# Weight chunks loaded as 112, 8 and 8 rows instead of 128

## The chip, the core and the metric

The kernel runs on one NeuronCore of a Trainium2 chip. The metric is the device time of one execution in microseconds. Before the change it is 1829.98 us, the median of three runs (1827.36 to 1831.81).

## The reference

The program computes a block of four mixers (convolution, short convolution, attention, recurrence) and an MLP, and then a second model of two layers on 16 meta tokens and 256 tokens of width 1024, all in float32. Nearly all of the time goes into the second part. Each of its layers ends in a retrieval of experts:

```python
def peer(h, w_query, sub_keys, u, v):
    # 8 heads, product keys (2 x 128 sub-keys), top-16 experts of 16384 for each head and token
    q = jnp.einsum('btd,dq->btq', hx, w_query)
    ...
    gate = jax.nn.softmax(best_s, axis=-1)
    u_sel = jnp.take(u, expert, axis=0)
    v_sel = jnp.take(v, expert, axis=0)
    act = jax.nn.gelu(jnp.einsum('btd,bthkd->bthk', hx, u_sel), approximate=False)
    return jnp.einsum('bthk,bthkd->btd', (gate * act), v_sel)
```

Between the two retrievals stand the key, value and query projections (w_kv, w_q), a stick-breaking attention, its output projection (w_o), and the queries of the second retrieval (peer_wq).

## The kernel before, in words

The 256 tokens are two tiles of 128. The retrieval of both layers is one loop over 32 units of 16 slots, 512 slots in all (`peer_gpsimd`, `peer_vector`, `peer_scalar`, `peer_tensor`). One slot is one expert for each of 128 pairs of token and head. GpSimd gathers for it 128 rows of 8 KB, the expert's u and v side by side (L634), into one of 8 buffers. VectorE multiplies the u half by the tokens' rows and sums (L675). ScalarE makes the gated weight from the sum (L706, L710). TensorE multiplies the weights with the v half (L662) and signals `v_used`, which frees the buffer for gather n + 8.

The work between the retrievals is spread over the same loop (`attend_pe`, `attend_act`, `attend_dve`), tile 0 beginning at step 34 of the 128 steps of four slots and tile 1 at step 66. Its weights come in chunks of 128 rows x 1024 columns, 512 KB: 48 chunks a tile (8 each for queries, keys, values and output, 16 for the retrieval's queries), 96 in all. They go through a ring of six buffers, `ring_w` (`RING_W`, L33). SyncE issues them in the order of their use: for chunk c >= 6 it first waits until TensorE has used chunk c - 6 (`w_used`), then issues one transfer (L1653) that adds 16 to the semaphore of that buffer. `product` (L821) waits on that semaphore for 16 times the number of chunks so far in this buffer, and then multiplies (L824, L828), at most one chunk ahead of each slot's value product in TensorE's order.

The same SyncE queue holds before these chunks the loads of the first block and of the keys, and after them the stores of the result (L1660), each behind a wait for its rows. All transfers, those of SyncE (queue 1), the gathers of GpSimd (queue 0) and the loads of instructions (queues 8 and 14), run on the same 16 DMA engines.

Other transfers that the prediction speaks of: the two loads of in_vectors, of 90 and 42 rows of 512 bytes (L1228, L1229); two loads of 16 rows of 4 KB (L1615, L1616); and eight copies of 16 rows of 4 KB within the SBUF (L1626).

Of the kernel before, what the change touches and what calls it, by code (L numbers as in the profile page):

```python
# [12 lines left out]
P = 128  # L13
# [19 lines left out]
RING_W = 6  # L33
# [19 lines left out]
def program(nc, x, vectors, w_in, lru_wa, lru_wx, w_out, post_mix_g, mlp_w1, mlp_w2, post_mlp_g, meta_tokens, norm_ffn,  # L53
            pool_w, pool_scale, w_kv, w_q, w_o, peer_wq, peer_keys, peer_uv, out):
    ctx = ExitStack()
    with ctx:
# [5 lines left out]
        def S(name):  # L62

            if name not in named:
                named[name] = nc.alloc_semaphore(name=name)
                count[name] = 0
            return named[name]
# [60 lines left out]
        def bank(b, n=1):  # L128
            return ps[:, BANK * b:BANK * (b + n)]
# [68 lines left out]
        ring_w = [big[:, W + D * i:W + D * (i + 1)] for i in range(RING_W)]  # L198
# [258 lines left out]
        def scores_ready(dve, u):  # L457

            if u == META_UNIT:
                return  # L460
            if u < L0_UNITS:
                dve.wait_ge(S("ffn0_scores_out"), u + 1)
            else:
                _, t, _, half = UNITS[u]
                dve.wait_ge(S("f_scores_out"), 2 * t + half + 1)
# [343 lines left out]
        def attend_tiles(t):  # L809

            return [X_TILES[0], META_TILE] if t == 0 else [X_TILES[1]]

        def product_done(engine, t, chunk):

            engine.wait_ge(S("w_used"), CHUNKS * t + chunk + KD)

        def product(pe, t, chunk, k, src, b, meta_bank=None):

            m = nc.tensor
            c = CHUNKS * t + chunk + k  # L820
            pe.wait_ge(S(f"w{c % RING_W}_loaded"), 16 * (c // RING_W + 1))  # L821
            w = ring_w[c % RING_W]
            for half in range(2):
                last = m.matmul(bank(b + half), src, w[:, BANK * half:BANK * (half + 1)],  # L824
                                start=(k == 0), stop=(k == KD - 1))
            if meta_bank is not None:
                for half in range(2):
                    last = m.matmul(bank(meta_bank)[TOK * half:TOK * (half + 1), :], kv_in[0][:, k, 0:TOK],  # L828
                                    w[:, BANK * half:BANK * (half + 1)], start=(k == 0), stop=(k == KD - 1))
            last.then_inc(S("w_used"), 1)  # L830

        def attend_pe(pe, t, i, q):
# [23 lines left out]
            for k in share(AT_Q, i)[q:q + 1]:  # L856
                product(pe, t, C_Q, k, q_in[:, k, :], 4)
# [4 lines left out]
            for k in share(AT_K, i)[q:q + 1]:  # L862
                product(pe, t, C_K, k, x_in[:, k, :], 6, 4 if t == 0 else None)
# [13 lines left out]
            for k in share(AT_V, i)[q:q + 1]:  # L877
                product(pe, t, C_V, k, x_in[:, k, :], 6, 4 if t == 0 else None)
# [118 lines left out]
        def attend_act(act, t, i):  # L997
# [13 lines left out]
            if i == AT_Q + 1:  # L1011
                if t == 1:
                    act.wait_ge(S("f_q_t"), 2)
                product_done(act, t, C_Q)
                a.activation(raw, bank(4, 2), ACT.Copy)
                a.activation(sq, bank(4, 2), ACT.Square).then_inc(S("a_raw"), 1)
            if i == AT_K + 1:
                product_done(act, t, C_K)
                act.wait_ge(S("a_scaled"), ONE["a_scaled"] * t + 1)
                if t == 0:  # L1020
                    a.activation(raw_m, bank(4)[0:HD], ACT.Copy)
                    a.activation(kn_m, bank(4)[0:HD], ACT.Square)
                a.activation(raw, bank(6, 2), ACT.Copy)
                a.activation(sq, bank(6, 2), ACT.Square).then_inc(S("a_raw"), 1)
# [23 lines left out]
            if i == AT_V + 1:  # L1048
                product_done(act, t, C_V)
                if t == 0:  # L1050
                    for half in range(2):
                        a.activation(v_meta[:, BANK * half:BANK * (half + 1)],
                                     bank(4)[TOK * half:TOK * half + META], ACT.Copy)
                a.activation(hn[:, t, :], bank(6, 2), ACT.Copy).then_inc(S("a_v_out"), 1)
# [552 lines left out]
        with nc.Block() as block:  # L1607
            @block.sync
            def _(sp):
                w1_v = mlp_w1[0].rearrange("(k p) n -> p k n", p=P)  # L1610
                w2_v = mlp_w2[0].rearrange("(f p) n -> p f n", p=P)
                wq_v = peer_wq[0].rearrange("(k p) n -> p k n", p=P)
                pool_v = pool_w[0].rearrange("g (k p) n -> p (g k) n", p=P)
                sp.dma_start(meta_poolw, pool_v).then_inc(S("meta_poolw_loaded"), 16)
                sp.dma_start(meta_scale, pool_scale[0].partition_broadcast(META)).then_inc(S("meta_gains_loaded"), 16)  # L1615
                sp.dma_start(meta_gain, norm_ffn[0].partition_broadcast(META)).then_inc(S("meta_gains_loaded"), 16)  # L1616
                sp.dma_start(w2b[1], w2_v[:, FT:2 * FT, :]).then_inc(S("w2_1_loaded"), 16)
                sp.dma_start(wq_peer, wq_v).then_inc(S("peer_wq0_loaded"), 16)
                sp.wait_ge(S("meta_mixed"), 1)
                sp.dma_start(meta_keys.rearrange("p j n -> p (j n)"), peer_keys[0]).then_inc(S("meta_keys_loaded"), 16)  # L1620
                for c in range(2, CHUNKS_MLP):
                    b = c % 2
                    if c == 3:
                        sp.wait_ge(S("meta_q_done"), 1)
                        for head in range(PH):
                            sp.dma_start(meta_x[META * head:META * (head + 1), :], meta_rows).then_inc(S("meta_x_loaded"), 16)  # L1626
                    sp.wait_ge(S("up_done"), FT * (c - 1))
                    sp.dma_start(w1b[b], w1_v[:, :, CHUNK * c:CHUNK * (c + 1)]).then_inc(S(f"w1_{b}_loaded"), 16)
                    sp.wait_ge(S("down_done"), FT * (c - 1))
                    sp.dma_start(w2b[b], w2_v[:, FT * c:FT * (c + 1), :]).then_inc(S(f"w2_{b}_loaded"), 16)  # L1630
                sp.wait_ge(S("meta_summed"), 1)
                sp.dma_start(wq_peer, wq_v).then_inc(S("peer_wq0_loaded"), 16)
                sp.wait_ge(S("up_done"), DFF // P - FT)
                sp.dma_start(scale_row, pool_scale[0].partition_broadcast(P)).then_inc(S("pool_w_loaded"), 16)
                sp.dma_start(poolw, pool_v).then_inc(S("pool_w_loaded"), 16)
                sp.wait_ge(S("mlp_done"), NT)
                sp.dma_start(ffn0_row, norm_ffn[0].partition_broadcast(P)).then_inc(S("ffn0_gain_loaded"), 16)
                sp.wait_ge(S("x2"), NT)
                sp.dma_start(gb[:, :, :].rearrange("p a n -> p (a n)"), peer_keys[0]).then_inc(S("keys0_loaded"), 16)
                sp.wait_ge(S("ffn0_scores_done"), L0_UNITS)  # L1640
                sp.dma_start(gb[:, 0, :], norm_ffn[1].partition_broadcast(P)).then_inc(S("gain0_loaded"), 16)

                kv_v, p_v = w_kv.rearrange("(k p) n -> k p n", p=P), peer_wq[1].rearrange("(k p) n -> k p n", p=P)
                q_v, o_v = (w[0].rearrange("(k p) n -> k p n", p=P) for w in (w_q, w_o))
                for c in range(NT * CHUNKS):
                    n, k = c % CHUNKS // KD, c % KD
                    if c == RING_W:
                        sp.wait_ge(S("experts_ready"), PH)
                        sp.dma_start(sc[:, 0:2 * PH * KEYS], peer_keys[1]).then_inc(S("keys1_loaded"), 16)
                    if c >= RING_W:  # L1650
                        sp.wait_ge(S("w_used"), c - RING_W + 1)
                    src = (q_v[k], kv_v[k, :, 0:D], kv_v[k, :, D:2 * D], o_v[k], p_v[k, :, 0:D], p_v[k, :, D:2 * D])[n]
                    sp.dma_start(ring_w[c % RING_W], src).then_inc(S(f"w{c % RING_W}_loaded"), 16)  # L1653

                out_v = out[0].rearrange("(t p) d -> p t d", p=P)
                for t in range(NT):
                    for g in range(QUADS):
                        r = slice(TOK * g, TOK * (g + 1))
                        sp.wait_ge(S("tile_out"), QUADS * (NT + t) + g + 1)
                        sp.dma_start(out_v[r, t, :], h[r, t, :]).then_inc(S("out_stored"), 16)  # L1660
                sp.wait_ge(S("out_stored"), 16 * NT * QUADS)
# [386 lines left out]
```

## Time and profile before

| what | value |
|---|---|
| median of 3 runs | 1829.98 us |
| profiled execution, first to last instruction | 1826.5 us |
| TensorE busy | 1366.8 us (75%) |
| VectorE busy | 1169.7 us (64%) |
| ScalarE busy | 597.3 us (33%) |
| GpSimd busy | 551.0 us (30%) |
| moved by DMA | 681.29 MB, mean 373 GB/s |
| mean granted TensorE clock | 0.843 |

The profile is of one execution. Its span leaves out what lies before the first and after the last instruction, so it is a little under the measured time. The page cuts the span into 40 slices of 45.7 us; a digit is the busy share in tenths. A DMA share of 1.00 or a little over means that the 16 engines have a packet in hand all the time. "A <- B" in the tables of waits means that the instruction A stood idle until B was done.

### The profile page before, as it was taken

The page shows a single profiled execution, that of the slowest core. Times are in us where ns is not written, and L with a number is a line of the kernel's source. Part 1 is how long each engine was busy: PE and PEld are TensorE (multiplying, and loading weights), DVE is VectorE, ACT ScalarE, POOL GpSimd, SP SyncE. Part 2 cuts the span into 40 slices and gives each one's busy share as a digit, 9 for nine tenths or more (in the row PEclk, how much of TensorE's full clock was granted, in tenths as well). Part 3 has the DMA queues.
Part 4 walks back from the last instruction along what each step waited for, and adds up shares of the span by engine and source line. Part 5 has one row for each costly group of instructions (what it writes and reads, how often), then busy time and mean ns, then how long its engine had stood idle before and what let it go on. Part 6 is the DMA issues. An engine that isn't in the chain of part 4 may idle for free.

```text
span 1826.5 us, 21618 instructions
## 1 busy us (share of the span) xinstructions
PE 1366.8 (75%) x7080; PEld 550.5 (30%) x7080; DVE 1169.7 (64%) x2705; ACT 597.3 (33%) x1530; POOL 551.0 (30%) x633
## 2 busy tenths in 40 slices
PE   8999999988874545698678865776787765655566
PEld 7856666653430010122122221221232210101011
DVE  5831334277776777656786647767877577677764
ACT  2421011124342323433443323433443333333332
POOL 2001232023332333322433224322342333333331
PEclk9999999999996676799777878897898977666677
DMA  9048697559999999999999999999999999999997
GB/s 358 5 176 345 204 373 263 230 211 419 420 420 419 417 415 417 420 417 409 417 392 418 416 418 406 419 417 416 384 410 418 420 421 421 421 422 418 418 421 292
DMA packets 118194, 681.29 MB, mean 373 GB/s; under 512 B 11790, under 2 KB 13970, under 8 KB 50114
## 3 DMA queue, kind: packets, MB, share of 16 engines
q0 software_dynamic: 78336, 553.68, 73.6%
q1 hardware_dynamic: 39745, 126.23, 18.0%
q8 instruction: 56, 0.92, 0.2%
q14 instruction: 57, 0.46, 0.1%
HBM read 678.30 MB, written 1.05 MB: 372 GB/s over the span
## 4 chain that ended last, share of the span: by engine, by line
DMA 37%; PE 29%; DVE 13%; ACT 4%; issue 3%; DVEq 3%; POOL 2%; ACTq 1%; POOLq 0%
DMA big<-in_peer_uv,expert 33%; PE ps L662 7%; DVE big L675 6%; PE ps L1900 6%; PE ps L1889 6%; PE ps L824 5%; DMA normed<-in_peer_uv,expert 5%; DVEq L528 2%; POOL big L634 2%; PE ps L647 2%; DVE residual L722 1%; ACT placed L706 1%; ACT L706 1%; ACT placed L710 1%; ACT L683 1%
## 5 line engine op out<-in xcount | busy, mean ns | idle before, releaser
L662 PE MATMUL ps<-big,placed 128*32 128x512 f32 x1992 | 596.1, 795 | 393.9 <-ACT placed L710 391.8
L675 DVE CUSTOM_DVE_ANT_0 big<-big,ps 128x1024 f32<-128x1024 f32 x498 | 595.7, 1219 | 340.4 <-DMA big<-in_peer_uv,expert 322.9
L634 POOL DMA_INDIRECT big<-in_peer_uv,expert x498 | 473.8, 951 | 1016.7 <-PE ps L662 855.9
L706 ACT ACTIVATE placed<-sel,dots 128x32 f32<-128x32 f32 x512 | 163.5, 319 | 797.2 <-DVE dots L675 789.6
L662 PEld LDWEIGHTS ps<-big,placed 128*32 128x32 f32 x1992 | 80.8, 122 | 820.5 <-ACT placed L710 734.7
L824 PE MATMUL ps<-big 128*128 128x512 f32 x384 | 187.2, 624 | 2.5 <-DVE big L1129 1.4
L710 ACT ACTIVATE placed<-placed,gate 128x32 f32<-128x32 f32 x512 | 164.6, 321 | 35.4 <-issue 0.3
L1900 PE MATMUL ps<-big,sc 128*128 128x512 f32 x256 | 115.5, 595 | 0.0
L1889 PE MATMUL ps<-ua,big 128*128 128x256 f32 (+1 forms) x512 | 110.4, 370 | 2.9 <-PEq L75 2.9
L824 PEld LDWEIGHTS ps<-big 128*128 128x128 f32 x384 | 69.8, 196 | 116.6 <-issue 108.7
L1889 PEld LDWEIGHTS ps<-ua,big 128*128 128x128 f32 x512 | 94.1, 194 | 27.8 <-issue 17.7
L1725 ACT ACTIVATE sc<-ps 128x256 f32<-128x256 f32 (+1 forms) x32 | 11.8, 370 | 173.2 <-PE ps L1889 173.2
L1517 PE MATMUL ps<-sc,big 128*128 128x256 f32 x288 | 63.6, 379 | 1.9 <-DMA big<-in_w_in 1.6
L349 PE MATMUL ps<-big 128*32 128x256 f32 x1024 | 61.5, 394 | 3.6 <-DVE big L278 3.6
L1900 PEld LDWEIGHTS ps<-big,sc 128*128 128x128 f32 x256 | 48.0, 190 | 49.5 <-issue 48.1
L1517 PEld LDWEIGHTS ps<-sc,big 128*128 128x128 f32 x288 | 54.0, 189 | 11.0 <-DVE sc L1367 2.1
L611 POOL DMA_INDIRECT big<-in_peer_uv,expert x32 | 38.9, 1216 | 60.4 <-DVE expert L572 26.6
L706 ACT ACT_TABLE_LOAD x40 | 51.3, 1283 | 1.1 <-issue 0.5
L722 DVE TENSOR_TENSOR residual<-residual,ps 32x512 f32<-32x512 f32 x64 | 43.7, 684 | 2.4 <-PE ps L662 0.5
L647 PE MATMUL ps<-ident,big 128*32 128x128 f32 x960 | 43.6, 326 | 0.4 <-DVE dots L675 0.4
L675 DVE DVE_READ_ACCUMULATOR2_ANT dots<- 128x1 f32 x512 | 42.2, 82 | 0.0
L647 PEld LDWEIGHTS ps<-ident,big 128*32 128x32 f32 x960 | 36.1, 130 | 18.1 <-issue 10.3
(371 smaller groups left out, 1280.2 us busy)
## 6 DMA issues: line engine op xcount, KB each, us to landing
big<-in_mlp_w SPq DMA_DIRECT2D x16, 2048.0 KB, 15.9
big<-in_peer_wq SPq DMA_DIRECT2D x2, 8192.0 KB, 26.9
big<-in_w_kv SPq DMA_DIRECT2D x32, 512.0 KB, 14.2
big<-in_peer_wq SPq DMA_DIRECT2D x32, 512.0 KB, 13.2
big<-in_w_in SPq DMA_DIRECT2D x5, 2048.0 KB, 17.8
big<-in_peer_uv,expert POOLq DMA_INDIRECT x530, 15.0
big<-in_w_q SPq DMA_DIRECT2D x16, 512.0 KB, 14.0
big<-in_w_o SPq DMA_DIRECT2D x16, 512.0 KB, 10.3
```

Of the source, the lines that this page charges most:

```text
L349: last = nc.tensor.matmul(bank(4 + u % 2)[TOK * j:TOK * (j + 1), 0:256], hnt[:, k, at:at + TOK], wq_peer[:, k, cols:cols + 256], start=(k ...
L634: nc.gpsimd.indirect_dma_start(out=pair_row(n), out_offset=None, in_=rows, in_offset=bass.IndirectOffsetOnAxis(ap=expert[:, n // TOPK % DE ...
L647: last = nc.tensor.matmul(to[TOK * j:TOK * (j + 1), :], hnt[:, k, at:at + TOK], ident[:], start=True, stop=True)
L662: last = nc.tensor.matmul(acc[r:r + TOK, :], placed[:, n % RING, :], pair_row(n)[:, D + BANK * half:D + BANK * (half + 1)], start=(opens a ...
L675: nc.vector.tensor_tensor_reduce(out=row, in0=row, in1=rows_x, scale=1.0, scalar=0.0, op0=ALU.mult, op1=ALU.add, accum_out=dots[:, u % 2, ...
L706: a.activation(to, sel32[:], ACT.Gelu, scale=dots[:, u % 2, k:k + 1])
L710: a.activation(to, to, ACT.Copy, scale=gate[:, u % DEEP, k:k + 1]).then_inc(S(f"weights_ready{UNITS[u][0]}"), 1)
L722: last = v.tensor_tensor(to, to, bank(group % 2)[r:r + TOK, :], ALU.add)
L824: last = m.matmul(bank(b + half), src, w[:, BANK * half:BANK * (half + 1)], start=(k == 0), stop=(k == KD - 1))
L1517: last = m.matmul(bank(b)[:, T * c:T * (c + 1)], win[chunk][:, k, P * (at + c):P * (at + c + 1)], ht[:, k, :], start=(k == 0), stop=(k == ...
L1889: last = m.matmul(bank(4 + q % UP_BANKS)[:, first:T], w1b[c % 2][:, k, P * (q % FT):P * (q % FT + 1)], h2t[:, k, first:T], start=(k == 0), ...
L1900: last = m.matmul(bank(2 * t + half), act2[:, q % FT, P * t:P * (t + 1)], w2b[c % 2][:, q % FT, BANK * half:BANK * (half + 1)], start=(q = ...
```

## The change

The load of a chunk is cut by rows into three transfers that add to the same semaphore, each by 16. The wait in `product` asks for the sum over the chunks so far in this buffer, 48 for each instead of 16. The order of issue, the ring, the bytes and the computation are the same.

```diff
+        def weight_parts(c):
+
+            return (0, 112), (112, 120), (120, P)
+
+        def weight_loads(c):
+
+            return 16 * sum(len(weight_parts(i)) for i in range(c % RING_W, c + 1, RING_W))
+
...
-            pe.wait_ge(S(f"w{c % RING_W}_loaded"), 16 * (c // RING_W + 1))
+            pe.wait_ge(S(f"w{c % RING_W}_loaded"), weight_loads(c))
...
-                    sp.dma_start(ring_w[c % RING_W], src).then_inc(S(f"w{c % RING_W}_loaded"), 16)
+                    for lo, hi in weight_parts(c):
+                        sp.dma_start(ring_w[c % RING_W][lo:hi], src[lo:hi]).then_inc(S(f"w{c % RING_W}_loaded"), 16)
```

## Rows read from the trace of the kernel before

**Rows 1.** The page's 40 slices: DMA busy tenths, and GB/s.

```profile
DMA  9048697559999999999999999999999999999997
GB/s 358 5 176 345 204 373 263 230 211 419 420 420 419 417 415 417 420 417 409 417 392 418 416 418 406 419 417 416 384 410 418 420 421 421 421 422 418 418 421 292
```

**Rows 2.** Busy time by stage: window, length, engines, TensorE clock, DMA share, GB/s.

```profile
400.00:549.00 149.00, 123.03 (x1444) 54.37 (x1436) 117.01 (x302) 58.20 (x174) 55.89 (x60) 0.94 1.01 420
549.00:880.00 331.00, 210.98 (x910) 52.24 (x912) 226.33 (x528) 115.37 (x291) 107.45 (x114) 0.78 1.01 416
880.00:970.00 90.00, 67.26 (x321) 20.13 (x318) 74.22 (x182) 38.71 (x115) 32.35 (x34) 0.73 1.00 405
970.00:1260.00 290.00, 207.66 (x944) 66.64 (x942) 184.41 (x431) 100.34 (x242) 87.48 (x93) 0.86 1.01 416
1260.00:1345.00 85.00, 61.55 (x347) 22.98 (x343) 74.52 (x154) 41.25 (x108) 32.14 (x32) 0.80 0.98 394
1345.00:1480.00 135.00, 104.34 (x513) 34.59 (x512) 85.51 (x207) 48.18 (x121) 42.14 (x45) 0.87 1.02 419
1480.00:1800.00 320.00, 188.05 (x764) 33.07 (x760) 227.25 (x530) 103.75 (x284) 119.57 (x128) 0.69 1.01 420
```

**Rows 3.** Gathers of 1480 to 1800 us, their landing, and the waits there.

```profile
L634 POOL DMA_INDIRECT big<-in_peer_uv,expert x128: 932/937/1199, 1479.4 to 1798.8; - x128
DMA to landing us min/median/max: 10.2/15.6/17.7
...
PEld ps L662 <- ACT placed L710: 267.5, 118, 6.5
ACT placed L706 <- DVE dots L675: 205.0, 107, 7.1
POOL big L634 <- PE ps L662: 188.2, 94, 5.8
...
DVE big L675 <- DMA big<-in_peer_uv,expert: 78.6, 73, 2.3
```

**Rows 4.** The page's DMA queues: packets, MB, share of 16 engines' span.

```profile
q0 software_dynamic: 78336, 553.68, 73.6%
q1 hardware_dynamic: 39745, 126.23, 18.0%
q8 instruction: 56, 0.92, 0.2%
q14 instruction: 57, 0.46, 0.1%
```

**Rows 5.** DMA issues by line: the two loads of vectors.

```profile
gain_rows<-in_vectors SPq DMA_DIRECT2D x1, 45.0 KB
gain_rows<-in_vectors SPq DMA_DIRECT2D x1, 21.0 KB
```

**Rows 6.** Issues at L1653: ns min/median/max of one, first and last start.

```profile
L1653 SPq DMA_DIRECT2D big<-in_w_q x16: 327/328/432, 549.1 to 1165.3; - x16
```

**Rows 7.** What SyncE's queue waited for: total, times, longest, in us.

```profile
SPq L1653 <- PE ps L824: 687.1, 74, 134.0
```

**Rows 8.** Issues at L1653 from 1163 to 1240 us, and their landing.

```profile
...
L1653 SPq DMA_DIRECT2D big<-in_w_o x6: 327/328/328, 1225.6 to 1238.8; - x6
L1653 SPq DMA_DIRECT2D big<-in_w_q x2: 328/328/328, 1163.6 to 1165.3; - x2
...
DMA to landing us min/median/max: 8.4/17.0/20.6
```

**Rows 9.** What ended TensorE's idle time before L824, 1163 to 1260 us.

```profile
  DMA big<-in_w_kv: 4.1, 5
```

**Rows 10.** Busy time in three short windows of the first block, columns as above.

```profile
136.00:138.00 2.00, 2.00 (x14) 1.52 (x13) 0.30 (x1) 1.13 (x4) 1.56 (x7) 1.00 1.13 278
187.40:192.60 5.20, 5.20 (x20) 3.53 (x19) 1.66 (x3) 0.00 (x0) 0.00 (x0) 1.00 0.62 101
140.00:141.00 1.00, 1.00 (x7) 0.74 (x6) 0.00 (x0) 0.00 (x0) 0.74 (x5) 1.00 1.11 434
```

## Prediction

> **What bounds the kernel now.** I read the forty slices first, because they hold the copy engines' load beside the compute. From the eleventh slice, a little before 400 us, the DMA line reads 9 in every slice and the rate stays near 420 GB/s until the last one [rows 1]. The table by stage says the same with one digit more: 420 GB/s at a share of 1.01 where only gathers run (400 to 549 and 1480 to 1800), 416 to 419 where weight chunks run beside them, and two dips, 405 and 394 GB/s [rows 2]. No compute engine is full in the same stages: VectorE is busy 227 of the 320 us from 1480 to 1800, TensorE 188 [rows 2]. Then I read who waits for whom in that quiet stretch. 128 gathers (L634) are issued in 320 us, 2.50 us each; one moves 128 rows of 8 KB, 1.05 MB, and 1.05 MB at 420 GB/s is 2.50 us. A gather lands 15.6 us after its issue, six gather times, so eight slots are nearly always in flight; VectorE waits for it (78.6 us), ScalarE for VectorE, TensorE for ScalarE, and GpSimd for TensorE to free a slot [rows 3]. That is a closed ring whose slowest member is the copying. So from 400 to 1815 us the end is set by the work of the DMA engines, and, since a gather counts as landed only when all of its engines have done their rows, by the work of the one engine that has most. What the change does to the sum over engines matters little; what it does to the fullest engine matters in full.
>
> **How much room the others have.** The shortfall from 420 GB/s tells how long the engines stood idle on average: 331 us x 4/420 = 3.2, 90 x 15/420 = 3.2, 290 x 4/420 = 2.8, 85 x 26/420 = 5.3, 135 x 1/420 = 0.3, together 15 us [rows 2]. The instruction loads took 0.2% (queue 8) and 0.1% (queue 14) of 16 engines' 1826.5 us, 58 and 29 us of one engine's time, give or take 15 for the rounding [rows 4]. If an engine carries much of that, it is the fullest. No row says which.
>
> **The change, part by part.**
> *Bytes.* Unchanged: 96 chunks of 512 KB.
> *How many engines a transfer takes.* This is the step on which all hangs. The code gives the data rows of SyncE's 161 transfers; they come to 37,172, and the page counts 39,745 packets on queue 1 [rows 4]. The 2,573 left are one completion write for each engine of each transfer: 161 x 16 = 2,576, less three. The only transfers whose rows are no multiple of 16 are the two of in_vectors, 90 and 42 rows of 512 bytes (45 and 21 KB) [rows 5]. 15 engines for 90 and 14 for 42, the largest divisors up to 16, give just these three. By that, 112 rows take 16 engines with 7 rows each, and 8 rows take 8 engines with one row each. [...]
> *Load of an engine.* If both 8-row parts fall on the same eight engines, these get 7 + 1 + 1 = 9 rows of 4 KB a chunk where they had 8, and the other eight get 7. One engine moves 420/16 = 26.2 GB/s [rows 2], so a 4 KB row is 0.156 us. Over 96 chunks the low eight gain 96 x 0.156 = 15.0 us of work and the high eight lose as much. All of it falls between 549 and 1424 us, where the DMA engines are full; only the 15 us of idle time could hide any.
> *Completion writes.* The low eight do 3 a chunk for 1, 192 more. The nearest row is queue 1's mean packet: 18.0% of 29,224 us over 39,745 packets is 0.132 us [rows 4], an upper bound of 25 us since those packets carry kilobytes; the lower is 0. Four bytes are nearer the low end: I take 0.01 us, 2 us in all.
> *SyncE.* 192 more issues at 0.33 us (0.43 in the first burst) [rows 6] are 63 us on a queue that waits 687 us for TensorE at this line [rows 7]. The third part leaves about 1 us after the first. Nothing else is queued behind but the stores (L1660), which wait for the tiles. Cost 0; without that cover it would be 1 us a chunk on its landing.
> *Later weights.* L821 now waits for three parts, and behind it on TensorE stand the four value products of the step. In the burst from 1163 us, 24 chunks (16 of w_kv between the rows shown) go out at 3.1 us apiece and their landing time climbs to 20.6 us [rows 8], longer than six slots of 3.1 us, and TensorE already waits 4.1 us for them [rows 9]. When both queues have work an engine alternates packets, 8 x (0.156 + 0.312) = 3.7 us a chunk; with 9 rows it is 4.2 us, 11 us more at the burst's end. TensorE will wait for weights there. But while it waits the low engines are copying those weights or gathers, so this is the 15 us again and no second price; it would be a second one only if both queues ran dry.
> *SBUF side.* A 128-row chunk and a gather run together at 416 GB/s against 420, so they do not disturb each other [rows 2]. Narrow transfers do: in the 16-row copies at 187 us the engines are busy 0.62 for 101 GB/s, 163 at full share against 416, so a packet takes 2.6 times as long; at 136 us, where two 16-row loads from HBM mix with 128-row ones, the rate is 278 GB/s for 434 after them [rows 10]. An 8-row part is as narrow for its eight engines. Bounds: 0, if engines reach their row at different times and the 112-row part behaves like a 128-row one, and 2 x 96 x 0.156 x 1.6 = 48 us if each 8-row packet is stretched as at 187 us. Those copies went out back to back on idle rings; here every engine comes to its row behind its own backlog, and 112 rows reach nearly all partitions. I take 0 and keep 48 for the range. [...]
>
> **Sum.** 15 + 2 = 17 us on the fullest engine if it is one of the low eight. The profiled execution becomes 1826.5 + 17 = 1843.5 us; its median of 1829.98 lies 3.5 above the span, so 1847.
>
> **The rivals.**
> *Collisions (slower still).* As above with narrow packets stretched, and the 112-row part landing across other engines' partitions. Priced at half the bound: 17 + 24 = 41 us, 1871; at the full bound 1895. It decides once a packet of an 8-row part takes over 0.3 us in the loop. For it: [rows 10]. Against: those are the only narrow transfers seen, and none ran beside gathers.
> *Relief (faster).* The fullest engine carries instruction loads and is one of the high eight. Then the change takes 15 us from it, and the bound becomes the low eight, which gain 17 us but had room. With the mean idle time of 15 us as room that is +2; engines without such loads have more than the mean. With a room of 32 the gain would be the whole 15. Middle: room 23, gain 6, 1824. It decides where the low engines' room exceeds 17 us. For it: the 58 us of queue 8 are nearly four times the 15 us of idle time, so they can't all lie on an engine that is not the fullest. Against: no row places them.
> *No effect.* The 8-row parts go round over all engines, or the load otherwise evens out: 2 x 96 more completion writes on half the engines at most, 1830 to 1832. [...] The three missing completion writes speak against it.
>
> **How the numbers follow.** Forecast 1847 with 0.33. Collisions 0.27, all slower. Relief 0.24: 0.19 faster, 0.05 the same. No effect 0.13: 0.10 the same, 0.01 faster, 0.02 slower. The last 0.03, slower by something else. That is 0.20 faster, 0.15 the same, 0.65 slower, with 0.2% (3.7 us), about what a measurement of this kernel can tell from no change, as the bound. The range runs from the relief case, 1822, to the full price of the narrow packets, 1895; some 0.1 is left on each side.
>
> **What would show it.** Queue 1 should count 96 x (8 + 8) = 1,536 more packets, the additional completion writes. The rate between 770 and 880 and between 1160 and 1260 should fall below 416 GB/s by more than in the quiet stretch, since the high eight idle; from 1480 on all is as before. TensorE's wait for weight chunks should grow from 4 us to tens. If the rate holds and the span shrinks, relief is right. If queue 1's packets grow much longer than 0.13 us on average, it is collisions. The forecast is wrong if the 8-row parts do not share their engines, or if the fullest engine is one of those relieved.

## The result, and the profile after

The changed kernel takes 2010.28 us (median of four runs, 2008.04 to 2013.5); the kernel before takes 1830.62 us beside it. The ratio is 1.0987, with a 95% interval from 1.0971 to 1.1003. The change makes the kernel 180 us slower. The forecast was 1847, and the range ended at 1895.

I read the slices first, as for the kernel before. From the page after:

```profile
DMA  9157787299999999999999999999999999999997
GB/s 330 59 209 261 303 325 281 97 421 419 420 323 419 413 421 394 296 281 347 384 370 331 295 326 379 329 289 284 395 364 322 308 370 410 417 421 413 420 421 304
```

Before, both lines were flat from the eleventh slice on [rows 1]. Now only the DMA digit is flat. The rate breaks down to 323 in the twelfth slice, which holds the first six chunks, and lies between 281 and 395 from the seventeenth slice to the thirty-third. Where only gathers run it is back at 410 to 421. The copy engines have a packet in hand all the time and move less.

The table by stage of the kernel after (window, length, busy time of the engines, clock, DMA share, GB/s; the columns of [rows 2]) says it with a digit more:

```profile
549.00:790.00 241.00, 128.29 (x572) 27.68 (x572) 166.40 (x396) 77.96 (x206) 81.46 (x86) 0.68 1.01 399
790.00:960.00 170.00, 116.51 (x428) 33.10 (x428) 82.46 (x193) 47.26 (x117) 36.06 (x39) 0.84 0.99 313
960.00:1030.00 70.00, 52.46 (x259) 17.85 (x258) 57.08 (x133) 30.97 (x90) 24.55 (x26) 0.73 0.98 395
1030.00:1275.00 245.00, 157.29 (x678) 48.69 (x677) 130.31 (x305) 68.08 (x169) 63.52 (x67) 0.75 1.00 335
1275.00:1340.00 65.00, 38.88 (x85) 11.50 (x84) 22.13 (x52) 13.98 (x29) 9.66 (x11) 0.79 1.02 294
1340.00:1600.00 260.00, 177.47 (x794) 59.46 (x792) 155.94 (x349) 87.82 (x220) 71.10 (x72) 0.81 1.00 332
1600.00:1980.00 380.00, 225.37 (x993) 44.93 (x992) 260.89 (x606) 121.55 (x330) 135.59 (x144) 0.71 1.01 409
```

Read the last two columns together. In the stages with many chunks the share stays between 0.99 and 1.02 while the rate is 294 to 335, against 394 to 419 in the stages with chunks before [rows 2]. No compute engine is full in them: from 1030 to 1275 us TensorE is busy 157 of 245 us, though its granted clock is 0.75 there. One stretch serves below for comparisons, 790 to 960 us, where every variant that splits tile 0's chunks loads them. The kernel before has there:

```profile
790.00:960.00 170.00, 133.77 (x613) 40.85 (x613) 120.51 (x276) 69.17 (x180) 53.19 (x55) 0.84 1.00 408
```

So at the same share the rate falls from 408 to 313: a byte occupies the engines 1.30 times as long.

The page's queues after (packets, MB, share of 16 engines' span):

```profile
q0 software_dynamic: 78336, 553.68, 73.0%
q1 hardware_dynamic: 41281, 126.24, 18.9%
```

These two lines hold nearly the whole answer. A packet is here one row of a transfer (4 KB of a chunk, 8 KB of a gather) or one completion write of four bytes: queue 0 has 8,704 records of four bytes in both traces, sixteen for each of 544 gathers, and queue 1 has 2,573 before and 4,109 after. A share times the span is the time that an average engine had packets in hand. After, it is (73.0% + 18.9%) x 2007.9 = 1845.3 us; before, (73.6% + 18.0%) x 1826.5 = 1673.1 us [rows 4]. The difference is 172 us of the 181 by which the span grew, for the same bytes. 122 us of it are on queue 0, whose gathers were not touched (1465.8 against 1344.3), and 51 us on queue 1 (379.5 against 328.8). Queue 1 counts 41,281 - 39,745 = 1,536 more packets.

The packets' own records in the two traces say it one by one. Of those that start between 790 and 960 us, a gather's 8 KB packet took 312 ns before and 401 ns after (medians), a chunk's 4 KB packet 160 and 221 ns. Both kinds became longer, at the same size.

Then the waits of the kernel after from 790 to 1345 us (who waited for whom: us in total, times, longest):

```profile
POOL big L634 <- PE ps L662: 398.7, 97, 13.8
ACT placed L706 <- DVE dots L675: 265.9, 98, 9.5
DVE big L675 <- DMA big<-in_peer_uv,expert: 216.3, 80, 6.9
PEld ps L662 <- ACT placed L710: 159.7, 74, 7.3
```

The ring is the one of [rows 3], with the copying as its slowest member still: VectorE waits 216 us of these 555 for gathers, GpSimd for a buffer to come free.

Last, who waits for the chunks. What ended TensorE's idle time before the product (L832 after, L824 before), over the whole kernel after:

```profile
  DMA big<-in_w_kv: 162.4, 53
...
  DMA big<-in_peer_wq: 78.1, 30
  DMA big<-in_w_q: 17.5, 5
...
  DMA big<-in_w_o: 3.1, 2
```

That is 261 us (weight loads and matmuls of TensorE added up, so partly the same time), where the burst before had 4.1 [rows 9]. It is tempting to take this for the cause. But the copy engines are busy all through it (share 0.98 to 1.02 in the table by stage), so it is the place where the lost rate shows, and no second loss.

### The profile page after: what moved, and what is told of

Its sections match the earlier page's. It is cut to its first block, busy times and chain, and to the rows that moved or that the text cites. A ratio compares the mean times of both kernels' runs of the same rounds, so it can differ in the third digit from the quotient of the medians.

```text
span 2007.9 us, 21810 instructions
## 1 busy us (share of the span) xinstructions
PE 1425.2 (71%) x7080; PEld 565.9 (28%) x7080; DVE 1171.3 (58%) x2705; ACT 597.3 (30%) x1530; POOL 552.1 (27%) x633
## 3 DMA queue, kind: packets, MB, share of 16 engines
q0 software_dynamic: 78336, 553.68, 73.0%
q1 hardware_dynamic: 41281, 126.24, 18.9%
## 4 chain that ended last, share of the span: by engine, by line
DMA 48%; PE 25%; DVE 10%; ACT 4%; issue 3%; DVEq 2%; POOL 2%; ACTq 0%; SPq 0%; POOLq 0%
DMA big<-in_peer_uv,expert 30%; DMA big<-in_w_kv 10%; PE ps L662 6%; DMA normed<-in_peer_uv,expert 6%; PE ps L1909 6%; PE ps L1898 5%; DVE big L675 5%; PE ps L832 3%; DMA big<-in_peer_wq 2%; POOL big L634 2%; DMA big<-in_w_o 2%; PE ps L647 1%; DVEq L528 1%; DVE residual L722 1%; ACT placed L706 1%
## 5 line engine op out<-in xcount | busy, mean ns | idle before, releaser
L662 PE MATMUL ps<-big,placed 128*32 128x512 f32 x1992 | 612.1, 822 | 414.1 <-ACT placed L710 412.6
L832 PE MATMUL ps<-big 128*128 128x512 f32 x384 | 220.7, 712 | 113.6 <-DMA big<-in_w_kv 69.2
L832 PEld LDWEIGHTS ps<-big 128*128 128x128 f32 x384 | 76.3, 216 | 247.1 <-DMA big<-in_w_kv 93.2
L647 PE MATMUL ps<-ident,big 128*32 128x128 f32 x960 | 47.9, 351 | 2.4 <-DVE dots L675 2.4
```

The costliest lines, as they stand in the source:

```text
L647: last = nc.tensor.matmul(to[TOK * j:TOK * (j + 1), :], hnt[:, k, at:at + TOK], ident[:], start=True, stop=True)
L662: last = nc.tensor.matmul(acc[r:r + TOK, :], placed[:, n % RING, :], pair_row(n)[:, D + BANK * half:D + BANK * (half + 1)], start=(opens a ...
```

## The experiments

In all of them the DMA share from 790 to 960 us stays between 0.98 and 1.02, so a run's loss can be read as time of the copy engines. The ratios are to runs of the kernel before on the same chip; its medians there were 1827.6 to 1831.1 us. The functions `weight_parts` and `weight_loads` are those of the change, the latter counting 16 for each part. A partition is one of the 128 rows of the SBUF, the memory on the chip: row r of a chunk goes to partition r. "Theory A" of the expectations says that a row is dear when another engine writes its partition than in a gather, B that more transfers and later completion cost, C that narrow 8-row parts do, D that the uneven load of the engines does. A strange or foreign row is in theory A a row that another engine writes; crowding is many engines at once on few partitions. Which engine writes which partition was not shown: a packet's record has its queue, time and size, and neither its engine nor its partition. What the expectations work out from it are the author's estimates.

**How a transfer is cut, first round.** Two transfers of 128 rows, one for each half of the columns; two of 112 and 16 rows; two halves of 64 rows; and the 112-row part alone.

e1_columns:

```diff
+        def weight_parts(c):
+            return (0, BANK), (BANK, D)
...
+                    for lo, hi in weight_parts(c):
+                        sp.dma_start(ring_w[c % RING_W][:, lo:hi], src[:, lo:hi]).then_inc(S(f"w{c % RING_W}_loaded"), 16)
```

> Each chunk is loaded by two transfers of 128 rows, the left and the right 512 columns: more transfers and 96 more issues and later last parts, but every row's partition is served as in a 128-row transfer. Theory A (which engine writes which partition: a split of the rows other than the 128-row one sends rows through engines that do not serve these partitions in a gather, and both slow down): no change, within 5 us of 1830. Theory B (more transfers for a chunk, later completion, TensorE waiting): a good part of the 180 us, 1870 or more. Theory C (the narrow 8-row parts, four engines to the same few partitions): no change. Theory D (nine rows on eight engines, seven on the others): no change.

Measured: 1841.97 us, ratio 1.0066 [1.0049, 1.0083], 12 us. Its queues:

```profile
q0 software_dynamic: 78336, 553.68, 73.1%
q1 hardware_dynamic: 53569, 126.24, 18.5%
```

(73.1% + 18.5%) x 1840.9 = 1686 us in hand, 13 more than before: 12,288 more data packets of half the size and 1,536 completion writes. A second transfer with its wait and its completion costs at most these 12 us. The change's 180 must come from the cut by rows. Theory A had allowed 5 us. The rest is the shorter rows: from 790 to 960 us a 2 KB packet took 89 ns on average, where a 4 KB one took 163 before, so two take 15 ns more, and 768 such pairs on each engine make 11.5 us.

e2_112_16:

```diff
+        def weight_parts(c):
+            return (0, 112), (112, P)
```

> Each chunk as 112 and 16 rows: every engine has 7 + 1 = 8 rows, so no engine has more than another; no 8-row part is left, but the 16-row part is as narrow for its 16 engines. Theory A: nearly all of the loss stays, 1990 to 2015. Theory B: two transfers for three, two thirds or less of the loss. Theory C: narrow packets as many as before (16 rows a chunk), about 2010. Theory D: the loss is gone but for what is not imbalance; if the imbalance were all of it, 1830.

Measured: 1976.19 us, ratio 1.0802 [1.0778, 1.0826], 147 us. From 790 to 960 us:

```profile
790.00:960.00 170.00, 121.31 (x438) 33.79 (x436) 87.33 (x201) 50.09 (x124) 39.05 (x40) 0.80 1.02 326
```

Queue 1 has 4,109 four-byte records here, 1,536 more than before, so each of the two transfers has sixteen completion writes. Read as one for each engine, as in the prediction, that is an estimate of seven rows and one for each, eight as before. With the load even by that estimate, four fifths of the loss are still there. Theory A's 1990 to 2015 was too much by 14 us; B (at most two thirds of the loss), C (about 2010) and D (1830 if uneven load were all) are further off.

e3_64_64:

```diff
+        def weight_parts(c):
+            return (0, 64), (64, P)
```

> Each chunk as 64 and 64 rows, four rows for each of 16 engines in either part: no narrow part, no imbalance. Theory A: a loss that depends on how many rows come through another engine than in a gather. [...] Theory C and D: 1830. Theory B: as the two transfers by columns.

Measured: 2010.8 us, ratio 1.0991 [1.0969, 1.1013], 182 us. From 790 to 960 us:

```profile
790.00:960.00 170.00, 116.72 (x420) 32.09 (x418) 81.35 (x192) 46.77 (x114) 35.35 (x38) 0.81 1.02 307
```

Two even halves with no narrow part cost as much as the change. So narrow parts are not needed for the loss. For theory A the author had estimated half of the loss, 1910 to 1930, and it missed.

e4_only_112 (the last 16 rows of each chunk are not loaded; the products use what the buffer holds):

```diff
+        def weight_parts(c):
+            return ((0, 112),)
```

> Only the first 112 rows of each chunk are loaded, in one transfer; the last 16 rows are left out, so the projections use old data there and the output differs. One transfer a chunk as in the kernel before, an eighth less weight data (96 x 64 KB, 15 us at 420 GB/s). Theory A: most of the loss stays, 1950 to 1990. Theory B, C and D: 1815 to 1830, faster than before by the bytes left out.

Measured: 1923.85 us, ratio 1.0516 [1.0493, 1.0538], 95 us slower although an eighth of the weights is left out. Those are one row of 0.156 us for each engine and chunk, 15 us, so a 112-row part costs some 110 us more than the same rows in a 128-row transfer. It is one transfer for each chunk, with 16 completion writes as before; nothing is left but which rows it holds. Here too theory A had the direction and not the size (1950 to 1990). With old data in 16 rows the second retrieval can pick other experts, but the gathers are as many and as large, and the rate is already low in the stretch of tile 0:

```profile
790.00:960.00 170.00, 125.36 (x484) 35.49 (x478) 100.93 (x239) 58.10 (x144) 42.65 (x45) 0.80 1.01 357
```

**What one more small transfer costs, by where it lands.** Now the chunk stays whole, and eight more rows of it are loaded into a buffer that nobody reads. The source, the size and the number of packets (41,281 on queue 1) are the same in the four runs; only the eight target partitions differ.

In e6_extra_own (`slot` is c % RING_W) the targets are eight partitions that are 4 apart:

```diff
                     sp.dma_start(ring_w[slot], src).then_inc(S(f"w{slot}_loaded"), 16)
+                    sp.dma_start(spare[32 * (slot // 4) + slot % 4:32 * (slot // 4) + 32:4], src[112:120]).then_inc(S(f"w{slot}_loaded"), 16)
```

> Each chunk is one transfer of 128 rows again, and beside it 8 of its rows are loaded once more, to a buffer that nothing reads, in partitions 0, 4, .. 28 (and the like for the other slots of the ring). Eight engines get 9 rows a chunk, the others 8. [...] This is the cost of load on eight engines alone: 96 x 0.156 = 15 us if the fullest engine is among the eight, 1844; less than 5 us if it is not. Theory A (which engine writes which partition) expects nothing beyond that; the theory that an 8-row transfer itself is dear expects 1850 or more.

Measured: 1845.47 us, ratio 1.009 [1.0073, 1.0107], 16 us.

e8_extra_other shifts them by 64 partitions:

```diff
+                    sp.dma_start(spare[64 + 32 * (slot // 4) + slot % 4:64 + 32 * (slot // 4) + 32:4], src[112:120]).then_inc(S(f"w{slot}_loaded"), 16)
```

> [...]

Measured: 1865.46 us, ratio 1.0197 [1.0179, 1.0214], 36 us: 20 more than e6. The author had estimated 10 more for theory A, and none for every other.

e5_extra_narrow takes eight in a row:

```diff
+                    sp.dma_start(spare[8 * slot:8 * slot + 8], src[112:120]).then_inc(S(f"w{slot}_loaded"), 16)
```

> As the two others, but the extra 8 rows go to 8 partitions side by side (0 to 7, 8 to 15, ..), four engines to each group of four. Theory A with crowding: dearest of the three, 10 to 25 us over the one with each engine in its own partitions. Theory C (narrow parts are the cause): one narrow part where the changed kernel has two, so half of the 180 us, 1920. Theory D (load alone): as the first of the three.

Measured: 1872.97 us, ratio 1.0237 [1.022, 1.0255], 43.5 us, far from the 1920 of theory C.

e11_extra_shifted shifts those of e6 by 4:

```diff
+                    sp.dma_start(spare[4 + 32 * (slot // 4) + slot % 4:36 + 32 * (slot // 4):4], src[112:120]).then_inc(S(f"w{slot}_loaded"), 16)
```

> The chunk stays one transfer of 128 rows. [...] Theory of the foreign group (an engine is slowed when it writes partitions that another engine fills in the gathers): the load of eight engines as in e6, 15 to 16 us, and 15 to 35 more for 768 foreign packets, as in e8: 1860 to 1880. Rival, that only the other half of the SBUF is dear (e8's rows lay there): as e6, 1842 to 1848.

Measured: 1862.76 us, ratio 1.0175 [1.0158, 1.0192], 32 us.

The stretch from 790 to 960 us of e6, e8 and e11, in this order:

```profile
790.00:960.00 170.00, 132.70 (x597) 40.32 (x596) 114.90 (x262) 67.36 (x176) 49.47 (x53) 0.82 1.00 402
```

```profile
790.00:960.00 170.00, 130.23 (x587) 39.20 (x585) 108.47 (x250) 64.96 (x168) 47.70 (x50) 0.84 1.00 388
```

```profile
790.00:960.00 170.00, 131.35 (x588) 39.77 (x586) 109.31 (x250) 64.97 (x168) 48.16 (x51) 0.84 0.99 389
```

The packets' records agree. From 790 to 960 us nine in ten of the gathers' 8 KB packets take at most 319 ns in e6, as in the kernel before, 364 in e11 and 369 in e8: the extra rows of e11 and e8 slow some of the gathers' packets, those of e6 do not.

Two prices come apart here. The first is load. Eight rows for 96 chunks are 3.1 MB, or 7.5 us if all sixteen engines share them at 420 GB/s, and 15.0 us on the fullest if eight do. e6 costs 16, and its 1,536 more packets are 8 rows and 8 completion writes a chunk (3,341 four-byte records on queue 1 against 2,573). So eight engines share them, and they are, or include, the engines that end last. The second is place. The same packets cost 20 us more at e8's partitions and 16 more at e11's. Over the 96 packets of one engine that is 0.21 and 0.16 us for each, beside the 0.156 us that a 4 KB row takes; it is the price of a packet, part of which falls on gathers beside it. Only 4 partitions lie between e6 and e11, so the other half of the memory is not what is dear (in e11 only one row in eight of the last two buffers falls there, partitions 64 and 65). Eight partitions in a row (e5) cost 27.5 us more than e6, 0.29 us a packet.

**Is it paid packet by packet?** e7_tile1, the change for the second tile's 48 chunks alone:

```diff
+        def weight_parts(c):
+            return ((0, P),) if c < CHUNKS else ((0, 112), (112, 120), (120, P))
```

> The change for the 48 chunks of tile 1 alone; those of tile 0 are loaded whole. If the loss is paid packet by packet at each split chunk (theory A), half of it, 1915 to 1925, and the stages of tile 0 as before. If it comes from a state that a split chunk sets off, or from one burst, far from half.

Measured: 1923.47 us, ratio 1.0515 [1.0494, 1.0536], 94 us, half of the change's 180. Its stretches with whole chunks and with split ones:

```profile
790.00:960.00 170.00, 134.97 (x612) 41.19 (x610) 119.51 (x274) 67.93 (x179) 51.50 (x54) 0.84 1.00 407
1160.00:1400.00 240.00, 163.35 (x656) 55.68 (x656) 146.56 (x328) 81.71 (x198) 62.89 (x64) 0.79 0.99 329
```

In the stretch with whole chunks the rate is that of the kernel before (408), and with split ones it falls: the loss is paid at the split chunks.

**Which rows go together.** e9_every_second takes the even and the odd rows, 64 in each transfer, where e3 took halves:

```diff
+                    for lo in weight_parts(c):
+                        sp.dma_start(ring_w[c % RING_W][lo:P:2], src[lo:P:2]).then_inc(S(f"w{c % RING_W}_loaded"), 16)
```

> Each chunk as its even and its odd rows, 64 each, four for each of 16 engines, in partitions two apart. As in the split into halves there are two transfers of 64 rows and no imbalance, but each part reaches partitions all over the SBUF instead of one half. [...] If what counts is only that a part has 64 rows, 2011 again. If strange rows cost nothing and crowding all, 1835 to 1860.

Measured: 1829.74 us, ratio 1.0003 [0.9991, 1.0015], no difference. For theory A the author had estimated 1965 to 1985, by a guess of which engine takes which row that was not shown, and it missed. The outcome is also that of the rival in the last sentence of the expectation, crowding alone; it is taken up below. From 790 to 960 us:

```profile
790.00:960.00 170.00, 134.62 (x614) 40.99 (x612) 118.70 (x272) 67.96 (x178) 52.01 (x54) 0.82 1.00 408
```

e10_every_fourth takes four transfers of 32 rows that are 4 apart:

```diff
+                    for lo in weight_parts(c):
+                        sp.dma_start(ring_w[c % RING_W][lo:P:4], src[lo:P:4]).then_inc(S(f"w{c % RING_W}_loaded"), 16)
```

> [...] Four transfers for two: if the number of transfers costs anything of its own, dearer than the split in even and odd rows by 10 us or more; by theory A the same within 10 us.

Measured: 1828.4 us, ratio 1.0005 [0.9994, 1.0016], no difference either, with three more transfers for each chunk than the kernel before. From 790 to 960 us:

```profile
790.00:960.00 170.00, 129.99 (x612) 39.81 (x608) 119.97 (x276) 69.49 (x182) 52.44 (x56) 0.86 1.01 408
```

In these 170 us the median packets of e9 take 312 and 160 ns (8 and 4 KB), those of e10 311 and 159, as before the change; in e3 they take 441 and 227.

e12_quarters takes four of 32 adjacent rows:

```diff
+        def weight_parts(c):
+            return (0, 32), (32, 64), (64, 96), (96, P)
```

> A chunk as four transfers of 32 rows, 0 to 31, 32 to 63 and so on: as many transfers of the same size as in e10, but of adjacent rows instead of every fourth. Theory of the foreign group: all or nearly all rows are filled by another engine than in a gather, so at least the cost of the adjacent halves of e3: 1975 to 2070, and the rate from 790 to 960 us is 310 or less. Rival, that e3's cost comes from what halves do and not from who fills which partition: between 1826 and 1850, as e10.

Measured: 2007.58 us, ratio 1.0969 [1.0928, 1.1009], 176 us. The stretch and the queues of e12, and then the queues of e10:

```profile
790.00:960.00 170.00, 116.93 (x409) 32.24 (x408) 79.58 (x182) 45.63 (x111) 34.72 (x37) 0.81 1.02 306
...
q0 software_dynamic: 78336, 553.68, 73.4%
q1 hardware_dynamic: 44353, 126.25, 19.1%
```

```profile
q0 software_dynamic: 78336, 553.68, 73.6%
q1 hardware_dynamic: 44353, 126.25, 18.2%
```

The same number of packets, of the same size, in as many transfers: in e10 the engines have them in hand for 91.8% of 1825.9, 1676 us, in e12 for 92.5% of 2011.5, 1861 us. Number and size of transfers, issues on SyncE and completion writes cost nothing that can be measured (e10's ratio is 1.0005); the adjacent rows cost 176 us. e9 against e3 is the same pair with 64 rows.

**What the experiments say together.** What a transfer costs beside the gathers depends on where its rows land. At the same number of packets, of the same size, eight more rows cost 16, 32, 36 or 43.5 us by their partitions alone (e6, e11, e8, e5). Parts of 64 and 32 rows cost 182 and 176 us as blocks of adjacent rows (e3, e12), and nothing in strides of 2 and 4 (e9, e10). A gather writes all 128 partitions, with sixteen completion writes (queue 0's 78,336 packets are 544 gathers of 128 rows and 16 completion writes), and so does a 128-row chunk, and the two run side by side at 416 GB/s [rows 2]. Where a split costs, the gathers' 8 KB packets grow with the chunks': their median from 790 to 960 us is 312 ns before, 401 after, 414 in e2, 441 in e3 and 430 in e12, and 312 and 311 in e9 and e10. So queue 0 gained 122 us without being touched.

Why the place matters was not shown. Theory A's cause, that another engine writes the partition than in a gather, is the author's guess, since no record names the engine or the partition of a packet. The sizes estimated for it missed by 14 us in e2, 26 in e4, 81 in e3 and 135 in e9. What stands is the place itself, by e11, e8 and e5 against e6.

A second guess is crowding: sixteen engines at once on few partitions, as in an adjacent half or quarter. It would explain e3 and e12 beside e9 and e10. It can't be all, since e11 and e8 place their eight rows as far apart as e6 and pay 16 and 20 us more, and the 112-row part of e4 reaches nearly all partitions and pays 110. What share it has in e3, e12 and e5, no run separates.

Of the change's 180 us, by e4, e2 and e6: some 110 for the 112-row part, 37 for sixteen more rows in one transfer (147 - 110), 16 for the load on eight engines, and some 17 left for cutting the sixteen rows into two narrow parts. This takes the parts as additive, which no run tests; e5's one narrow part, at 27.5 us beyond its load, agrees with 37 + 17 = 54 for two.

## Why the prediction was wrong

**The bound (right).** The copying sets the end from 400 us on. The share stays between 0.98 and 1.02, and the time in hand explains 172 of the 181 us by which the profiled span grew.

**How many engines a transfer takes (right).** 1,536 more packets were predicted and counted. That eight rows go to eight engines is borne out by e6: eight completion writes for each of its 96 small transfers (3,341 four-byte records against 2,573), and 16 us, not 7.5. "The low eight" of the prediction are these eight, "the high eight" the others; which engines they are, no run shows.

**Load of an engine, 15.0 us (right).** e6 measures this term by itself at 16 us. With it the relief rival falls: the engines that an 8-row part loads are not ones with room.

**Completion writes, 2 us, and SyncE, 0 (right within what can be told).** e9 adds 1,536 completion writes and 96 issues, e10 three times as many of both, and both take the time of before. In the trace a four-byte packet takes 9 ns before, where the estimate was 0.01 us, and 12 after (medians, 790 to 960 us).

**Later weights, no second price (right).** TensorE's wait for weights did grow, from a few to 261 us, far beyond the tens expected. It is a wait for copy engines that were busy throughout (share 0.98 to 1.02). The alternation of packets that the prediction reckons with there can be counted in the trace before: from 1170 to 1250 us there are 3,044 packets on queue 0 and 3,051 on queue 1, one for one.

**SBUF side, 0 (wrong; this is the whole miss).** "112 rows reach nearly all partitions. I take 0 and keep 48 for the range" is the step that failed. The sum had 0 where the runs show some 110 us for the 112-row part (e4) and some 54 for the two narrow parts beyond their load, together about the 163 us between 1847 and 2010. The error was in what counts. I asked how many partitions a transfer reaches, as the 16-row copies of [rows 10] suggested, and 112 of 128 looked as good as all. e3 reaches just as many partitions in each transfer as e9, and pays 182 us to its 0: the number does not decide. The two differ only in which rows go together, and why that matters was not shown. The 420 against 416 GB/s of [rows 2] was read as "they do not disturb each other", which holds for whole chunks and for strided parts (e9, e10), and not for blocks of adjacent rows. The prediction even named "the 112-row part landing across other engines' partitions" in its rival, and then priced only the two 8-row parts, at 48 us at most. With a bound for all nine packets of a low engine by the same factor, 9 x 96 x 0.156 x 1.6 = 216 us, the range would have held the time.

**The rivals.** Collisions is right in its sign. Queue 1's packets were to grow, and they did, from 0.132 us (18.0% of 29,224 over 39,745) to 18.9% of 32,126 over 41,281 = 0.147 us, in spite of 1,536 more packets of four bytes. The larger part, the gathers' longer packets on queue 0, was not foreseen at all. It priced the two narrow parts at 24 to 48 us beyond their load, and they cost 37 + 17 = 54, a little above its bound; the 110 of the wide part it left out. No effect falls with the result. Two halves in blocks cost 9.9% (e3) and in alternating rows nothing (e9), with sixteen completion writes for each transfer in both (4,109 four-byte records on queue 1), so that sharing the engines is not what costs.

**What would show it.** The rate was to fall between 770 and 880 and between 1160 and 1260 us because half of the engines idle. It fell, to 313 and 335 in the stages around them, but with the share at 0.99 and 1.00: the engines did not idle. This pair of numbers alone separates load from collisions: engines that idle would show a lower share.

## What to carry to other kernels

When the DMA engines are the bound, split a transfer that runs beside others in regular strides over the partitions, or along the columns, not into blocks of adjacent rows: here strides of 2 and 4 were free, columns cost 0.7%, and blocks of 64 and 32 rows 10%. To price such an edit, count every packet of the transfer, not only those of the small parts, and put the ones in a place that no trace has yet shown beside the neighbouring traffic into the range at their full price. In a trace, a DMA share that stays full while GB/s fall is the sign; idle engines show as a falling share, as in the 0.62 of the copies in [rows 10].

None of the versions tried beats the kernel before; e10, with 32-row transfers in strides, equals it.

## What the runs showed of the hardware

- The place of a small transfer's rows changes its cost by a factor of two and more at the same bytes and number of packets: 16 us for rows 4 partitions apart that begin at partition 0, 32 when shifted by 4, 36 when shifted by 64, 43.5 for eight in a row (e6, e11, e8, e5).
- The cost falls on both sides: queue 0's untouched gathers took 122 us more of an average engine's time, queue 1 took 51; the median packets of 790 to 960 us went from 312 to 401 ns and from 160 to 221.
- It does not grow with the number of blocks: two adjacent halves, four adjacent quarters and the change all end within 2007 to 2011 us (e3, e12, after). Why the change meets the other two is open.
- Four transfers of 32 rows in the place of one of 128 are free (e10), while halving the row length to 2 KB costs 12 us (e1).
- Open is also whether the order of reading matters: in e9 and e10 against e3 and e12 source and target rows change together. e6, e8, e11 and e5 change the target alone, and show that the target is enough.
